# Conditioning pairs two steps earlier, VectorE's own units later, and a four-bank turn for the last heads, in a fused transformer block

## The chip, the core and the metric

The kernel runs on one core of a Trainium2 chip. The metric is device time in microseconds for one execution. Before the change the median of three runs is 1242.2 us (1241.29 to 1243.9).

## What is computed

One layer (D = 2048, 256 tokens, float32): a conditioning vector `c` gives six shift, scale and gate vectors through `w_ada`; the normalised and modulated input goes through one wide projection `w_in` into retention and attention heads; their mix goes through `w_out`; then a gated MLP with a short convolution, and a final norm with its own modulation.

```python
c_act = silu(c)
sh1, sc1, gt1, sh2, sc2, gt2 = split(c_act @ w_ada + b_ada, 6)
h = rms_norm(x, g_mix) * (1 + sc1) + sh1
rq, rk, rv, rg, aq, ak, av = split(h @ w_in + b_in)
mix = concat([retention(rq, rk, rv, rg), attention(aq, ak, av, sinks)]) @ w_out
x = x + gt1 * mix
h = rms_norm(x, g_ffn) * (1 + sc2) + sh2
a, b = split(h @ w_up)
x = x + gt2 * ((silu(conv3(a) + b_conv) * b) @ w_down)
fsh, fsc = split(c_act @ w_final_ada + b_final_ada)
y = rms_norm(x, g_final) * (1 + fsc) + fsh
```

## The kernel before

Every weight tile is split in two parts, `whi` (ScalarE, function `hi`, L661) and `wlo` (VectorE, function `lo`, L1017), and TensorE forms each product in three passes (L1546 to L1548). A piece of 128 x 1024 weights is a *step*; steps are numbered from 0 and go through TensorE in that order. Eight slots hold raw steps of the front (`front_in`), four hold the split ones. Each step of the front is one transfer of 512 KB, issued by SyncE (`load_step`, L368), and waits until the step eight before it is split (`lo_ready`).

The front, steps 0 to 51, needs the modulated input `h`, and each part of `h` needs a part of the conditioning. So the front is cut into *stages* of input tiles (`STAGE_K`: 2, 2, 4, 4, 4 tiles), and the conditioning into *jobs*. Job 0 has two parts of eight loads each (`first_units`, `first_pair`), job 1 gives the tiles of stage 2, job 2 those of stage 3, job 3 those of stage 4, job 4 a shift of the second half. A job has 16 *units* of 512 KB, loaded by GpSimd (`load_unit`, L535). TensorE takes them two at a time (`ada_pair`, L1677, eight small matmuls into bank 7 or 3); each pair counts up `ada_pe`, and GpSimd loads further units into the slots that this frees: unit 8 of job 1 waits for pair 0, and pair n of jobs 2 and 3 is asked for when the pair three before it is done (six slots). After pair 7 VectorE adds the bias (`pe_rows`, L1049), TensorE sums (`sum_columns`, L1619), VectorE forms scale and shift (`mod_cols`), and ScalarE and VectorE write the tiles of `h` of the next stage.

From job 5 on the conditioning is VectorE's own: one instruction of 1.28 us for each unit (`ada`, L1027), at the places that the table `UNIT_STEPS` gives: a number in it means that VectorE takes one unit right after `lo` of that step. Everything on one engine runs in the written order, so a unit that has not landed holds up all that is queued behind it on VectorE.

A stage has four groups of two retention heads (`two_heads`). A head takes one PSUM bank, `SPILL_BANK` says which, and VectorE adds the bank to what is kept in SBUF (`add_heads`, L1127; in stage 0 half of the heads go through `first_heads` on VectorE, L1111, and half on ScalarE). TensorE may start a head only when its bank is free (`bank_free`), that is, when VectorE or ScalarE has taken the head before it. The order of the step numbers: 0 and 2 are query steps, 1, 3, 4, 5 the heads of stage 0; 6 and 8 queries, 7, 9, 10, 11 the heads of stage 1; 12 to 23 are stage 2, 24 to 35 stage 3; 36 to 51 the rest, with the attention scores of batch 0 beside steps 44 to 47 (`att_scores`, L1811, and `scores_out` on VectorE, L1213). From step 52 on values, gates, output projection and MLP follow.

SyncE also waits for units of the conditioning between its own loads (`after_unit(job, k)`: go on when unit k of the job has landed), which sets in what order the two streams reach the DMA engines.

The functions and lines at stake:

## Time and profile before

| what | us |
|---|---|
| median of three runs | 1242.2 |
| lowest, highest | 1241.29, 1243.9 |
| the profiled execution's own time | 1238.36 |
| its span | 1236.6 |
| TensorE busy | 1182.4 (96%) |
| VectorE busy | 898.6 (73%) |

Share of the span in tenths, in 40 equal slices of 30.9 us each:

```profile
PE   5879899999999999999999999999999999999995
DVE  3334458789878797778878788787565665897886
DMA  9979899989787986788787888886565547797851
```

The span is the time from the first to the last instruction of one execution; 1.8 us of the execution's time lie around it. In the first slices TensorE is not full while the DMA engines are. A row of the timeline gives start, duration, engine, line, operation, output and inputs, shapes and the number of merged instructions; in square brackets the idle time before it and what ended it.

### The profile page before, as it was taken

What the parts mean: (1) busy time and instruction counts of PE and PEld (TensorE: products, weight loads), DVE (VectorE), ACT (ScalarE), POOL (GpSimd) and SP (SyncE); (2) the same over time, 40 slices, a digit from 0 to 9 for tenths busy, and PEclk for the clock granted to TensorE, in tenths of its full rate; (3) what the DMA queues carried; (4) which work ended last, traced back from release to release, by engine and by line L of the source; (5) the groups of instructions that cost most, each with busy time, mean ns of one, the idle gap of its engine ahead of it and who ended that gap; (6) DMA issues with size and microseconds to landing.
All of it is one profiled execution on the core that took longest, in us unless ns stands there. A gap on an engine that the chain in (4) does not pass through costs nothing.

```text
span 1236.6 us, 19629 instructions
## 1 busy us (share of the span) xinstructions
PE 1182.4 (96%) x6800; PEld 992.4 (80%) x6800; DVE 898.6 (73%) x1111; ACT 656.8 (53%) x947; POOL 180.4 (15%) x307
## 2 busy tenths in 40 slices
PE   5879899999999999999999999999999999999995
PEld 3757779876788788888888888888888887888774
DVE  3334458789878797778878788787565665897886
ACT  5313324473465446756666556566665555555652
POOL 6224132122121120011101011100000001020101
PEclk9889899999999999999999999999999999999998
DMA  9979899989787986788787888886565547797851
GB/s 314 356 281 391 299 338 328 376 341 391 283 308 282 350 311 208 237 283 292 273 292 268 292 276 283 281 279 218 174 200 175 199 181 279 273 366 258 302 180 68
DMA packets 167478, 342.73 MB, mean 277 GB/s; under 512 B 10266, under 2 KB 103552, under 8 KB 166784
## 3 DMA queue, kind: packets, MB, share of 16 engines
q1 hardware_dynamic: 129072, 206.13, 48.3%
q0 software_dynamic: 37536, 134.30, 29.4%
q10 hardware_dynamic: 816, 1.58, 0.4%
q8 instruction: 34, 0.56, 0.2%
q14 instruction: 20, 0.16, 0.0%
HBM read 339.87 MB, written 2.10 MB: 277 GB/s over the span
## 4 chain that ended last, share of the span: by engine, by line
PE 86%; DMA 6%; DVE 3%; issue 2%; ACT 1%; POOL 1%; DVEq 0%; ACTq 0%; POOLq 0%
PE ps L1570 26%; PE ps L1546 14%; PE ps L1575 14%; PE ps L1547 13%; PE ps L1548 13%; DMA arena<-in_w_ada 3%; PE ps L1677 2%; DMA ada_raw<-in_w_ada 2%; DMA raw<-in_w_in 1%; DVE acc L1027 1%; DVE xb L1344 1%; ACT whi L661 0%; POOL ada_raw L545 0%; DVE arena L1342 0%; PE ps L1852 0%
## 5 line engine op out<-in xcount | busy, mean ns | idle before, releaser
L668 ACT ACTIVATE whi<-raw 128x1024 fp32r<-128x1024 f32 x256 | 271.8, 1063 | 286.0 <-PE ps L1575 180.4
L1022 DVE TENSOR_TENSOR wlo<-raw,whi 128x1024 fp32r<-128x1024 f32 x256 | 311.8, 1223 | 104.0 <-ACT whi L668 104.0
L1570 PE MATMUL ps<-hh,whi 128*128 128x512 f32 x1408 | 353.0, 392 | 0.3 <-issue 0.3
L1570 PEld LDWEIGHTS ps<-hh,whi 128*128 128x128 f32 x1408 | 253.2, 189 | 45.8 <-issue 0.5
L1027 DVE SCALAR_TENSOR_TENSOR acc<-ada_raw,c_act,acc 128x1024 f32<-128x1024 f32 (+1 forms) x176 | 225.3, 1280 | 40.4 <-DMA ada_raw<-in_w_ada 35.0
L661 ACT ACTIVATE whi<-raw 128x1024 fp32r<-128x1024 f32 x124 | 130.6, 1059 | 217.0 <-PE ps L1548 178.2
L1546 PE MATMUL ps<-whi,hh 128*128 128x512 f32 x608 | 242.5, 399 | 1.3 <-DVE arena L1127 1.1
L1548 PE MATMUL ps<-whi,hh 128*128 128x512 f32 x608 | 237.6, 391 | 0.0
L1547 PE MATMUL ps<-wlo,hh 128*128 128x512 f32 x608 | 237.4, 391 | 0.0
L1575 PEld LDWEIGHTS ps<-hh,wlo 128*128 128x128 f32 x1408 | 192.1, 190 | 13.7
L1575 PE MATMUL ps<-hh,wlo 128*128 128x256 f32 x1408 | 196.3, 282 | 0.0
L1017 DVE TENSOR_TENSOR wlo<-raw,whi 128x1024 fp32r<-128x1024 f32 x124 | 150.8, 1220 | 60.2 <-ACT whi L661 60.2
L1546 PE MATMUL ps<-hh,whi 128*128 128x256 f32 x416 | 126.1, 303 | 22.2 <-DVE xb L1127 17.3
L1546 PEld LDWEIGHTS ps<-whi,hh 128*128 128x128 f32 x608 | 114.6, 188 | 32.4 <-issue 5.3
L535 POOL DMA_DIRECT2D ada_raw<-in_w_ada x132 | 74.0, 561 | 413.6 <-DVE acc L1027 357.1
L1548 PEld LDWEIGHTS ps<-whi,hh 128*128 128x128 f32 x608 | 114.5, 188 | 24.6
L1547 PEld LDWEIGHTS ps<-wlo,hh 128*128 128x128 f32 x608 | 114.5, 188 | 23.6 <-issue 0.7
L1547 PE MATMUL ps<-hh,whi 128*128 128x256 f32 x416 | 122.0, 293 | 0.0
L1548 PE MATMUL ps<-hh,wlo 128*128 128x256 f32 x416 | 121.9, 293 | 0.0
L1546 PEld LDWEIGHTS ps<-hh,whi 128*128 128x128 f32 x416 | 85.1, 205 | 43.7 <-issue 40.8
L1547 PEld LDWEIGHTS ps<-hh,whi 128*128 128x128 f32 x416 | 85.3, 205 | 0.0
L1548 PEld LDWEIGHTS ps<-hh,wlo 128*128 128x128 f32 x416 | 85.2, 205 | 0.0
(161 smaller groups left out, 820.4 us busy)
## 6 DMA issues: line engine op xcount, KB each, us to landing
raw<-in_w_up SPq DMA_DIRECT2D x176, 512.0 KB, 4.4
ada_raw<-in_w_ada POOLq DMA_DIRECT2D x140, 512.0 KB, 6.8
raw<-in_w_down SPq DMA_DIRECT2D x44, 1024.0 KB, 6.7
ada_raw<-in_w_final_ada POOLq DMA_DIRECT2D x64, 512.0 KB, 5.3
arena<-in_w_ada POOLq DMA_DIRECT2D x52, 512.0 KB, 8.7
raw<-in_w_in SPq DMA_DIRECT2D x52, 512.0 KB, 8.0
raw<-in_w_in SPq DMA_DIRECT2D x16, 1024.0 KB, 9.4
raw<-in_w_out SPq DMA_DIRECT2D x16, 1024.0 KB, 7.1
```

The source lines that it names most:

```text
L535: pool.dma_start(dst, src).then_inc(ada_in[slot], 16)
L661: nc.scalar.activation(whi[:, step % RING, :], raw_of(step), ACT.Copy).then_inc(hi_ready, 1)
L668: nc.scalar.activation(whi[:, i % RING, :], raw_of(step0 + i), ACT.Copy).then_inc(hi_ready, 1)
L1017: nc.vector.tensor_tensor(wlo[:, step % RING, :], raw_of(step), whi[:, step % RING, :], ALU.subtract).then_inc(lo_ready, 1)
L1022: nc.vector.tensor_tensor(wlo[:, i % RING, :], raw_of(step0 + i), whi[:, i % RING, :], ALU.subtract).then_inc(lo_ready, 1)
L1027: nc.vector.scalar_tensor_tensor(a, w, c_col, a, ALU.mult, ALU.add).then_inc(ada_acc, 1)
L1546: nc.tensor.matmul(out_ap, lhs[0], rhs[0], start=start, stop=False, skip_group_check=skip)
L1547: nc.tensor.matmul(out_ap, lhs[0], rhs[1], start=False, stop=False, skip_group_check=skip)
L1548: return nc.tensor.matmul(out_ap, lhs[1], rhs[0], start=False, stop=True, skip_group_check=skip)
L1570: nc.tensor.matmul(bank_of(m), whi[:, slot, tile(m, j)], hh[:, k0 + j, :, :].rearrange("p i s -> p (i s)"), start=start and j == 0, stop=F ...
L1575: last = nc.tensor.matmul(bank_of(m)[:, 0:S], wlo[:, slot, tile(m, j)], hhi[:, k0 + j, :], start=False, stop=True, skip_group_check=True)
L1677: last = nc.tensor.matmul(ps[row:row + 32, bank, :], c_pad[:, k, :], ada_of_slot(slot)[:, b * 512:(b + 1) * 512], start=n == 0, stop=True, ...
```

## The change

Seven edits, all in the front:

- `ada_pair(1, 0)` stands after `two_heads(0, 2, 0)` and the sums of job 0, between steps 4 and 5; it stood after step 6. Each later pair of job 1 moves with it. Its wait for `spill_dve` goes, since the heads of stage 0 no longer use bank 7.
- The heads of stage 0 take banks 5 and 6 in turn. VectorE's `first_heads(0)` stands before `lo(5)` and `lo(6)`, and `first_heads(1)` between `lo(8)` and `lo(9)`.
- SyncE issues step 5 with no wait, steps 6 and 7 after the unit 11 of job 0, step 9 with step 8, step 11 with step 10, and step 12 after unit 7 of job 1 in place of unit 12.
- VectorE's units in stage 2 move from steps 16, 18, 19, 21 to 19, 20, 23, 24, and in stage 3 from 28, 30, 31, 33, 35 to 31, 32, 34, 35, 37.
- The heads of stage 4 turn in banks 5, 6, 3, 4 instead of 5, 6, 4; the values' banks are (5, 6, 3, 4), the gates' (7, 3, 5, 6), retention's bank is 4, and the values' banks are read in the order 2, 0, 1, 3.
- `add_heads(4, ...)` of the first three groups stands after the scores of p = 7, after those of p = 9 and after the rotation of p = 11, where it stood before the scores of p = 6, of p = 8 and before the rotation of p = 10 (VectorE's p is step 42 + p).
- Nothing is computed in another way, and no instruction is added.

```diff
-SPILL_BANK = ((5, 6, 5, 6, 7, 5, 6, 7), (5, 6) * 4, (5, 6) * 4, (5, 6) * 4, (5, 6, 4, 5, 6, 4, 5, 6))
+SPILL_BANK = ((5, 6) * 4, (5, 6) * 4, (5, 6) * 4, (5, 6) * 4, (5, 6, 3, 4) * 2)
...
-AQ_BANK, AK_BANK, RV_BANKS, RG_BANKS, RET_BANK = (0, 1, 2, 4), 3, (3, 4, 5, 6), (7, 3, 4, 5), 6
+AQ_BANK, AK_BANK, RV_BANKS, RG_BANKS, RET_BANK = (0, 1, 2, 4), 3, (5, 6, 3, 4), (7, 3, 5, 6), 4
...
-UNIT_STEPS = ((16, 18, 19, 21), (28, 30, 31, 33, 35), range(38, 48), (49, 51, 53, 54), range(55, 66), (66, 66, 67, 67, 68, 69),
+UNIT_STEPS = ((19, 20, 23, 24), (31, 32, 34, 35, 37), range(38, 48), (49, 51, 53, 54), range(55, 66), (66, 66, 67, 67, 68, 69),
...
             load_heads(0, 2)
-            after_unit(0, 10)
             load_heads(0, 3)
-            after_unit(0, 13)
+            after_unit(0, 11)
             load_queries(2)
+            load_heads(1, 0)
             after_unit(0, 15)
-            load_heads(1, 0)
             load_queries(3)
-            after_unit(1, 2)
             load_heads(1, 1)
-            after_unit(1, 5)
+            after_unit(1, 3)
             load_heads(1, 2)
-            after_unit(1, 8)
             load_heads(1, 3)
-            after_unit(1, 12)
+            after_unit(1, 7)
...
-            for step in range(1, 7):
+            for step in range(1, 5):
                 lo(step)
             first_heads(0)
+            lo(5)
+            lo(6)
             first_rows(1)
             mod_cols(0, FIRST_BANKS[1], 0, 1)
             for k in STAGE_K[1]:
                 h_lo(k, 0)
+            lo(7)
+            lo(8)
             first_heads(1)
-            for step in range(7, 11):
-                lo(step)
+            lo(9)
+            lo(10)
             add_heads(1, 0)
...
-                if p in (6, 8, 10, 12):
-                    add_heads(4, p // 2 - 3)
                 if p == 12:
+                    add_heads(4, 3)
                     values_out()
...
+                    if p % 2:
+                        add_heads(4, p // 2 - 3)
...
             two_heads(0, 2, 0)
             first_sums(1)
+            ada_pair(1, 0)
             two_heads(0, 3, 0)
+            ada_pair(1, 1)

             att_queries(2)
-            ada_pair(1, 0)
+            ada_pair(1, 2)
             two_heads(1, 0, 0)
-            ada_pair(1, 1)
+            ada_pair(1, 3)
             att_queries(3)
-            ada_pair(1, 2)
+            ada_pair(1, 4)
             two_heads(1, 1, 0)
-            ada_pair(1, 3)
+            ada_pair(1, 5)
             two_heads(1, 2, 0)
-            for n in range(4, PAIRS):
-                ada_pair(1, n)
+            ada_pair(1, 6)
+            ada_pair(1, 7)
             sum_columns(1, ADA_BANK[1], 0)
             two_heads(1, 3, 0)
```

On TensorE, behind the heads of step 4, the sums of job 0 (the rows of `ones,acc`) and then step 5 stood before:

```order
L1646 MATMUL ps<-ones,acc 128x1 [waits ada_rows]
L1646 MATMUL ps<-ones,acc 128x1 x3
L1546 MATMUL ps<-hh,whi 128x256 [waits spill_dve,lo_ready,hlo_ready]
L1547 MATMUL ps<-hh,whi 128x256
L1548 MATMUL ps<-hh,wlo 128x256
```

and now, in the same place (the rows of `ada_raw,c_pad` are the first pair of job 1):

```order
L1650 MATMUL ps<-ones,acc 128x1 [waits ada_rows]
L1650 MATMUL ps<-ones,acc 128x1 x3
L1679 MATMUL ps<-ada_raw,c_pad 32x512 [waits ada_in0,mod_ready]
L1679 MATMUL ps<-ada_raw,c_pad 32x512
L1679 MATMUL ps<-ada_raw,c_pad 32x512 [waits ada_in1]
L1679 MATMUL ps<-ada_raw,c_pad 32x512
L1550 MATMUL ps<-hh,whi 128x256 [waits spill_act,lo_ready,hlo_ready]
L1551 MATMUL ps<-hh,whi 128x256
L1552 MATMUL ps<-hh,wlo 128x256
```

The pair stands before step 5, and the wait for ScalarE's head reads has taken the place of that for VectorE's.

On VectorE, in stage 2, from `lo(14)` on (`wlo` rows are `lo` of a step, `acc<-ada_raw` rows are its own units, `xb<-ps` and `gate<-ps` rows are `add_heads`), before:

```order
L1017 TENSOR_TENSOR wlo<-raw,whi 128x1024 x3
L1027 SCALAR_TENSOR_TENSOR acc<-ada_raw,c_act,acc 128x1024
L1017 TENSOR_TENSOR wlo<-raw,whi 128x1024
L1127 TENSOR_TENSOR xb<-ps,xb 128x512 x2
L1017 TENSOR_TENSOR wlo<-raw,whi 128x1024
L1027 SCALAR_TENSOR_TENSOR acc<-ada_raw,c_act,acc 128x1024
L1017 TENSOR_TENSOR wlo<-raw,whi 128x1024
L1027 SCALAR_TENSOR_TENSOR acc<-ada_raw,c_act,acc 128x1024
L1017 TENSOR_TENSOR wlo<-raw,whi 128x1024
L1127 TENSOR_TENSOR xb<-ps,xb 128x512 x2
```

and now:

```order
L1014 TENSOR_TENSOR wlo<-raw,whi 128x1024 x4
L1124 TENSOR_TENSOR xb<-ps,xb 128x512 x2
L1014 TENSOR_TENSOR wlo<-raw,whi 128x1024 x2
L1024 SCALAR_TENSOR_TENSOR acc<-ada_raw,c_act,acc 128x1024
L1014 TENSOR_TENSOR wlo<-raw,whi 128x1024
L1024 SCALAR_TENSOR_TENSOR acc<-ada_raw,c_act,acc 128x1024
L1124 TENSOR_TENSOR xb<-ps,xb 128x512 x2
L1014 TENSOR_TENSOR wlo<-raw,whi 128x1024 x3
L1024 SCALAR_TENSOR_TENSOR acc<-ada_raw,c_act,acc 128x1024
L1124 TENSOR_TENSOR gate<-ps,gate 128x512 x2
```

Ahead of the second `add_heads` of the stage (the second row of `xb<-ps`) stood three units; now two stand there, and the third follows `lo(23)`.

On VectorE, at p = 6, before (the rows of L1213 are the scores):

```order
L1017 TENSOR_TENSOR wlo<-raw,whi 128x1024
L1127 TENSOR_TENSOR arena<-ps,xb 128x512 x2
L1213 ISA arena,smx<-ps,arena 128x128
L1213 ISA smx 128x1
```

and now, at the end of p = 7 and the start of p = 8:

```order
L1214 ISA arena,smx<-ps,arena 128x128
L1214 ISA smx 128x1
L1124 TENSOR_TENSOR arena<-ps,xb 128x512 x2
L1014 TENSOR_TENSOR wlo<-raw,whi 128x1024
L1214 ISA arena,smx<-ps,arena 128x128
```

The two additions of a group of heads stand behind the scores and no longer ahead of them.

## Rows read from the trace of the kernel before

**Rows 1.** The page: busy time of TensorE; the chain that ended last, by engine.

```profile
PE 1182.4 (96%) x6800; PEld 992.4 (80%) x6800; DVE 898.6 (73%) x1111; ACT 656.8 (53%) x947; POOL 180.4 (15%) x307
PE 86%; DMA 6%; DVE 3%; issue 2%; ACT 1%; POOL 1%; DVEq 0%; ACTq 0%; POOLq 0%
```

**Rows 2.** Stretches: length, busy PE, PEld, DVE, ACT, POOL, granted clock, DMA share, GB/s.

```profile
22.90:45.70 22.80, 18.95 (x168) 15.52 (x160) 8.32 (x15) 8.71 (x14) 12.30 (x17) 0.93 1.00 350
45.70:63.20 17.50, 14.79 (x97) 13.21 (x98) 9.72 (x18) 8.39 (x13) 3.41 (x5) 0.80 0.88 323
63.20:82.60 19.40, 12.10 (x96) 9.12 (x96) 4.95 (x6) 3.18 (x3) 7.70 (x11) 0.91 0.77 271
99.40:128.60 29.20, 29.20 (x226) 21.93 (x225) 12.29 (x13) 9.54 (x10) 9.63 (x14) 0.99 1.03 391
134.80:140.80 6.00, 6.00 (x28) 5.31 (x32) 3.85 (x4) 0.50 (x1) 0.00 (x0) 0.51 0.93 315
140.80:160.00 19.20, 19.20 (x161) 17.63 (x154) 12.19 (x17) 9.52 (x14) 4.62 (x7) 1.00 0.57 187
```

**Rows 3.** Timeline of TensorE, steps 4, 10, 11 and the first pair of stage 2.

```profile
50.69 0.39 PE L1546 MATMUL ps<-hh,whi 128*128 128x256 f32 x1 [2.71 <-DVE xb L1111]
84.47 0.55 PE L1546 MATMUL ps<-hh,whi 128*128 128x256 f32 x1 [9.17 <-DVE xb L1127]
95.18 0.37 PE L1546 MATMUL ps<-hh,whi 128*128 128x256 f32 x1
102.60 1.06 PE L1677 MATMUL ps<-ada_raw,c_pad 128*32 128x512 f32 x8
```

**Rows 4.** Timelines of SyncE, ScalarE and VectorE: step 12 loaded, split in two.

```profile
76.45 0.34 SPq L368 DMA_DIRECT2D raw<-in_w_in  x1
81.41 1.06 ACT L661 ACTIVATE whi<-raw 128x1024 fp32r<-128x1024 f32 x1 [6.50 <-DMA raw<-in_w_in]
82.50 1.23 DVE L1017 TENSOR_TENSOR wlo<-raw,whi 128x1024 fp32r<-128x1024 f32 x1 [6.33 <-ACT whi L661]
```

**Rows 5.** Timelines of SyncE, ScalarE and VectorE: step 13, and job 1's bias.

```profile
82.57 0.88 SPq L368 DMA_DIRECT2D raw<-in_w_in  x2
86.51 1.06 ACT L661 ACTIVATE whi<-raw 128x1024 fp32r<-128x1024 f32 x1 [4.04 <-DMA raw<-in_w_in]
93.52 0.69 DVE L1049 TENSOR_TENSOR acc<-ps,acc 128x512 f32<-128x512 f32 x1 [2.38 <-PE ps L1677]
```

**Rows 6.** Timelines of VectorE and TensorE: units awaited, and heads that wait.

```profile
131.57 1.28 DVE L1027 SCALAR_TENSOR_TENSOR acc<-ada_raw,c_act,acc 128x1024 f32<-128x1024 f32 x1 [14.29 <-DMA ada_raw<-in_w_ada]
133.91 1.28 DVE L1127 TENSOR_TENSOR xb<-ps,xb 128x512 f32<-128x512 f32 x2
134.74 0.55 PE L1546 MATMUL ps<-hh,whi 128*128 128x256 f32 x1 [6.09 <-DVE xb L1127]
171.53 0.37 PE L1546 MATMUL ps<-hh,whi 128*128 128x256 f32 x1 [1.37 <-DVE xb L1127]
184.41 0.36 PE L1546 MATMUL ps<-hh,whi 128*128 128x256 f32 x1 [0.65 <-DVE xb L1127]
```

**Rows 7.** Timeline of TensorE: scores of batch 0 that wait for VectorE.

```profile
234.27 0.67 PE L1811 MATMUL ps<-arena 64*64 64x128 f32 x16 [0.90 <-DVE smx L1213]
243.49 0.67 PE L1811 MATMUL ps<-arena 64*64 64x128 f32 x16 [1.80 <-DVE smx L1213]
```

**Rows 8.** Timeline of TensorE: two neighbouring pairs of job 2.

```profile
118.88 1.06 PE L1677 MATMUL ps<-arena,c_pad 128*32 128x512 f32 x8
122.95 1.07 PE L1677 MATMUL ps<-arena,c_pad 128*32 128x512 f32 x8
```

**Rows 9.** DMA view of 82.6 to 201.5; GpSimd's unit loads of 30 to 140.

```profile
DMA packets 15159, 39.61 MB, mean 333 GB/s; under 512 B 1455, under 2 KB 3759, under 8 KB 15149
L535 POOL DMA_DIRECT2D ada_raw<-in_w_ada x20: 549/711/749, 33.7 to 129.7; - x20
DMA to landing us min/median/max: 3.9/8.9/15.1
```

More of the change, by code:

```diff
@@ L1247, in token_values @@
                 dve.wait_ge(step_done, STEP_RG)
-                for n in range(4):
+                for n in (2, 0, 1, 3):
                     t, b = n // 2, n % 2
@@ L1295, in _ @@
                     rotate(qT, 8 * 3 + 4, 0, p - 10)
+                if p == 11:
+                    add_heads(4, 2)
                 if p in (30, 34, 38):
@@ L1666, in ada_pair @@
                 if n == 0:
-                    if job == 1:
-                        pe.wait_ge(spill_dve, 8)
                     pe.wait_ge(mod_ready, 5 if job == JOB_SH2 else job)
@@ L1726, in bank_free @@
                 if stage == 0:
-                    return (None, None, (spill_act, 2), (spill_act, 4), (mod_ready, 1), (spill_dve, 2), (spill_dve, 4),
-                            (spill_act, 6))[n]
+                    return (None, None, (spill_act, 2), (spill_act, 4), (spill_dve, 2), (spill_dve, 4),
+                            (spill_act, 6), (spill_act, 8))[n]
                 if stage == 1 and n < 2:
-                    return ((spill_act, 8), (spill_dve, 6))[n]
+                    return spill_dve, 6 + 2 * n
                 if stage < 4 or n < 2:
                     return spill, 8 * (stage - 1) + n - 1
-                return (aq_ready, 8) if n == 2 else (spill, 8 * 3 + n - 2)
+                return ((aq_ready, 8) if n == 3 else (k2_ready, 5)) if n < 4 else (spill, 8 * 3 + n - 3)
             def two_heads(stage, group, i):
@@ L1864, in ret_values @@
                     .then_inc(o_ps, 1)
-            rv_free = [(k2_ready, 5), (spill, 30), (spill, 31), (spill, 32)]
+            rv_free = [(spill, 29), (spill, 30), (spill, 31), (spill, 32)]
             rg_free = [(mod_ready, 7), (v_ready, 1), (v_ready, 2), (v_ready, 3)]
```

## The prediction

> **What bounds the kernel now.** The page comes first. TensorE is busy for 1182.4 of 1236.6 us, and it makes 86% of the chain that ended last [rows 1]. So time can be had only where TensorE waits or runs at its lower clock, and the slices put most of that into the first 200 us. The stretches come next [rows 2]: up to 63 us and from 99 to 129 us the DMA engines move 323 to 391 GB/s and are full, but from 63.2 to 82.6 they move 271 and from 140.8 to 160.0 only 187. The front is bound by the DMA engines in turn with something that starves them. The timeline of TensorE names it. It idles 2.71 us in step 4, 9.17 us before step 10, 6.09 us before step 19, 1.37 and 0.65 us in stage 3, each time until VectorE has emptied a PSUM bank [rows 3, 6], and 0.90 and 1.80 us beside the scores [rows 7]. Behind each stands something else that VectorE waits for first: before step 10 it stands in `lo(12)`, whose data SyncE asked for only at 76.45 and which reached ScalarE at 81.41 [rows 4]; before step 19 it waits 14.29 us for a unit of its own job [rows 6]. The same waits cost clock: in the 6 us after the 6.09 us idle the granted clock is 0.51, which is the 1.2 GHz level, so some 2.9 us of those 6 are lost [rows 2, 6].
>
> **Part 1: the gate of stage 2 (pairs of job 1, SyncE's order, banks of stage 0).** Stage 2 can't start before all 16 units of job 1 have landed, been multiplied and summed. Before, SyncE issued steps 13 and on at 82.57, right behind the last unit [rows 5]. From 22.9 us on, what must land up to then is 8 loads of job 0's second part, 16 units and steps 1 to 12: 36 loads of 0.524 MB, 18.9 MB. The engines moved 350 x 22.8 = 7.98 MB and 323 x 17.5 = 5.65 MB by 63.2 [rows 2]; 5.24 MB are left. In the new order unit 8 is asked for once pair 0 is done, two steps earlier than now (6.1 us at full clock), so GpSimd's queue shouldn't run dry; at the 391 GB/s of the full stretch the rest takes 13.4 us, and the last unit lands at 76.6. If the dip at the end of the second stretch is filled as well it is 10.9 MB in 27.9 us, 73.6. If GpSimd's requests come late again it is 82.6, no gain. I take 76.6: TensorE needs until about 78 for steps 5 to 10 and eight pairs at 4.07 us for a step and a pair [rows 8], so asking and moving are nearly even.
>
> Then a new wait shows. TensorE has done pair 7 at about 78, but VectorE's `pe_rows(1)` stands behind `lo(13)`, and step 13 is still issued only when the last unit has landed. From the issue to ScalarE's start it took 3.9 us for step 13 and 5.0 for step 12, the one with units under way [rows 5, 4]; units of job 2 are under way now, so 5.0: 81.6. `hi` and `lo` end 2.3 us later (from 81.41 to 82.50 + 1.23) [rows 4], two additions take 1.2 (1.28 with their tails) [rows 6], and from `pe_rows` to step 11 it is 95.18 - 93.52 = 1.7 [rows 5, 3]. Step 11 starts at 76.6 + 5.0 + 2.3 + 1.2 + 1.7 = 86.8 instead of 95.18: 8.4 us earlier. TensorE has idled some 6 us by then. Steps 11 and 12 took 102.60 - 95.18 = 7.4 us now [rows 3], against 2 x (4.07 - 1.0) = 6.1 at full clock; after 6.09 us of idle the low clock lasted about 6 us more [rows 2], which makes up to 9.1. I take 8.5, 1.1 us worse. Part 1 gives 7.3 us, between 0 and 12.7 (73.6 and full clock). The 2.71 us wait of step 4 goes, since `first_heads(0)` no longer stands behind `lo(5)` and `lo(6)`; I count it at nothing of its own, because the DMA engines are the limit of this part. For the same reason steps 5 to 7, which SyncE asks for earlier, may make the last loads of job 0 up to 3 us late without moving the gate. The new wait of step 5 for ScalarE's head reads costs nothing: a pair of 1.06 us and the sums stand before it.
>
> **Part 2: VectorE's units in stages 2 and 3.** The third unit stood behind `lo(19)`, landed at 131.57 and held up the heads that free the bank for step 19. It now stands behind `lo(23)`, which can't run before TensorE has done step 19, 4 to 7 us behind the place where the wait hurt. Its load is still asked for after pair 4 of job 2, so in the same relation to TensorE, and lands in time by 1 to 3 us. The 6.09 us go, and with them the low clock: 2.9 us. In stage 3 the units go from steps 28, 30, 31 to 31, 32, 34, and 1.37 + 0.65 = 2.0 us go [rows 6]. No instruction is added; a unit of 1.28 us stands ahead of `mod_cols(2)` now and may make `h` 0.6 us later, hidden by two head steps of TensorE. Part 2 gives 11.0 us, between 2 and 11.
>
> **Part 3: last heads and banks.** The scores of p = 6 and p = 8 no longer stand behind two additions (1.2 us) and, at p = 8, behind a step of TensorE that isn't done. Both waits are covered by that: 0.90 + 1.80 = 2.7 us [rows 7], between 0 and 2.7. What is late next is the bank of step 50, which needs the additions of p = 9, now behind scores and maxima; they end about half a microsecond ahead of it. The values' first bank needs the additions of p = 11, done a step before it is used, and its third waits for p = 12 as now.
>
> **Part 4: what continuous running costs.** From 82.6 to 201.5 the engines moved 39.61 MB [rows 9]. At 391 GB/s that is 101.3 us, so from 76.6 it can't be done before 177.9, and TensorE would be at that point at 201.5 - 7.3 - 9.0 - 2.0 = 183.2. The margin is 5.3 us in 107. A pair of jobs 2 and 3 is asked for when the pair three before it is done, so three cycles take at least a pair, two issues of 0.71 us and the time to landing: with the median of 8.9 it is (1.07 + 1.42 + 8.9) / 3 = 3.8 us a cycle, under the 4.07 of TensorE, and from 9.7 us on the loads set the pace [rows 8, 9]. Unbroken running makes queues longer than the median. About ten pairs are paced so (five in each stage, the first three are asked for ahead). I take 10.6 us to landing, 0.3 us a pair, 3 us in all; nothing at the median, 18 us at the maximum of 15.1.
>
> **Sum.** 7.3 + 11.0 + 2.7 - 3.0 = 18.0. The profiled execution took 1238.4 (1236.6 of span and 1.8 around it), so the same execution would take 1220.4. It lies 3.8 below the median of 1242.2, and from the median I get 1224.2, about 1224.
>
> **A rule against it.** The full stretch of rows 2 shows 391 GB/s for 29 us. The Trainium skill (DMA: Bandwidth & Descriptors, Where 436 GB/s comes from) puts the limit for loads from HBM at about 358 GB/s for a core. By that page's figure, as an estimate, the 39.61 MB would need 110.6 us and end at 187.2, 4.0 us behind TensorE, which is close to the 3.0 of part 4. The trace doesn't agree with the page on the rate; it would have to fall with a longer full stretch.
>
> The trace shows step 12 landing 5 us after its issue with units under way and step 13 after 3.9 [rows 4, 5]. The Trainium skill (the same page, Queues, rings and completion order) says that each DMA engine takes turns between the queues that have work, so an earlier step of SyncE takes its share from the units whoever asked first. By that rule the early steps 5 to 7 delay job 0's last loads, which the sum takes at nothing because the total of bytes up to the gate is the same.
>
> **Rivals.** *The loads set the pace.* Landing takes about 12.5 us when nothing pauses: 5.0 us a pair, 0.93 x 10 = 9 us lost instead of 3. For it: the full stretch had 391 GB/s with no reserve. Against it: TensorE was busy for all 29.2 us of it. Time 1242.2 - 21.0 + 9.3 = 1230.5.
>
> *All gaps close.* The gate lands at 73.6, the clock stays up, no pair waits: 12.7 + 11.0 + 2.7 = 26.4, 1215.8. Against it: the wait behind step 13 is long enough for the clock to fall.
>
> *The gate doesn't move.* The early steps push back the loads that pair 0 needs and the last unit still lands near 82; then only parts 2 and 3 less part 4 are left, 10.7: 1231.5. For it: unit 8 can't be asked for before pair 0, and pair 0 stands behind all of job 0's loads. Against it: at 271 GB/s the engines had room from 63.2 to 82.6 [rows 2].
>
> *Slower.* The ring of six slots, with landing beyond what was seen. The gains make 21.0 at most by the sum, so ten pairs have to lose 2.1 us each, which starts at 3 x 6.17 - 2.5 = 16.0 us to landing. At 17 us it is 6.5 us a pair, 24 lost, 1245.5. The longest landing now is 15.1 [rows 9], of a unit queued behind others, so only if every load became like the worst.
>
> **Chances.** Forecast 0.58, the loads set the pace 0.18, all gaps close 0.11, the gate doesn't move 0.07, slower 0.06. The predicted time is 1224, its own range 1219 to 1229. The range for 8 in 10 takes in most of both neighbours: 1214 to 1233. About 0.2% (2.5 us) is what a measurement can tell from no change. Faster 0.91, same 0.03 (small parts of two rivals), slower 0.06.
>
> **What would show it.** No idle before step 10 ended by VectorE; one wait of 4 to 7 us instead, before the sums of job 1, behind `lo(13)`, with the low clock after it; step 11 near 87 and the first pair of stage 2 near 95. No 6 us wait in stage 2, and none on VectorE above a few us for its third unit; 375 to 390 GB/s where 187 was. Pairs of jobs 2 and 3 ended by a DMA, some tenths each. The scores' waits gone. I am wrong if step 11 starts after 92, if pairs in stage 2 follow each other at 4.6 us or more, or if a new wait on VectorE stands before steps 48 to 52.

## The result

The changed kernel takes 1221.19 us (median of four runs, 1220.77 to 1223.63) against 1241.74 (1237.94 to 1243.9, four runs): ratio 0.9842, 95% interval 0.9814 to 0.9869. The prediction was 1224, 1214 to 1233. In the profiled executions the span went from 1236.6 to 1219.6, 17.0 us; the prediction's sum was 18.0. The four runs of one kernel lie 3 to 6 us apart, so below the sizes of single parts are read from the profiles, at the same instruction in both.

The page of the changed kernel: the span, the busy time, and TensorE and the DMA engines in 40 slices.

```profile
span 1219.6 us, 19628 instructions
PE 1177.9 (97%) x6800; PEld 986.6 (81%) x6800; DVE 899.0 (74%) x1111; ACT 656.4 (54%) x947; POOL 180.6 (15%) x307
PE   5979999999999999999999999999999999999995
DMA  9999999999688894888878788886555457897841
```

TensorE's busy time fell by 4.5 us with the same 6800 matmuls: that is clock. The other 12.5 us are idle time that went. The DMA engines are now busy for 90% or more in each of the first ten slices.

Four stretches of the changed kernel (length, busy PE, PEld, DVE, ACT, POOL, granted clock, DMA share, GB/s), beside those of [rows 2]:

```profile
45.70:63.20 17.50, 15.96 (x134) 12.62 (x131) 10.16 (x17) 7.40 (x12) 7.70 (x11) 1.00 1.03 388
63.20:76.30 13.10, 12.26 (x99) 9.31 (x98) 6.08 (x7) 3.17 (x3) 4.88 (x7) 1.00 0.95 354
76.30:143.00 66.70, 59.94 (x456) 49.57 (x455) 35.99 (x46) 24.23 (x32) 19.95 (x29) 0.92 0.99 369
85.80:96.00 10.20, 10.20 (x56) 10.09 (x56) 5.00 (x10) 5.76 (x10) 1.46 (x2) 0.63 1.03 393
```

Where 323 GB/s were moved from 45.7 to 63.2 us at a clock of 0.80, there are 388 at full clock now (a second profile of the changed kernel, e10 below, has 388 at a clock of 0.90). After the gate of stage 2 the clock is low again, 0.63 for 10 us.

TensorE's timeline of the changed kernel, in the place of [rows 3]: step 10, pairs 6 and 7 of job 1, its sums, the first pair of stage 2.

```profile
74.06 0.36 PE L1550 MATMUL ps<-hh,whi 128*128 128x256 f32 x1 [0.84 <-DVE xb L1124]
77.11 1.92 PE L1679 MATMUL ps<-arena,c_pad 128*32 128x512 f32 x16
85.80 1.87 PE L1623 MATMUL ps<-pick,acc 128*128 128x2 f32 x8 [6.76 <-DVE acc L1046]
96.02 1.07 PE L1679 MATMUL ps<-ada_raw,c_pad 128*32 128x512 f32 x8
```

The 9.17 us before step 10 are 0.84. In their place stand 6.76 us before the sums. What VectorE did in that time is the chain forecast, in the places of [rows 4, 5] (SyncE, ScalarE, VectorE):

```profile
76.33 1.98 SPq L368 DMA_DIRECT2D raw<-in_w_in  x3
...
81.63 1.06 ACT L658 ACTIVATE whi<-raw 128x1024 fp32r<-128x1024 f32 x1 [9.58 <-DMA raw<-in_w_in]
...
82.72 1.23 DVE L1014 TENSOR_TENSOR wlo<-raw,whi 128x1024 fp32r<-128x1024 f32 x1 [8.21 <-ACT whi L658]
83.86 0.68 DVE L1124 TENSOR_TENSOR gate<-ps,gate 128x512 f32<-128x512 f32 x1
85.06 0.68 DVE L1046 TENSOR_TENSOR acc<-ps,acc 128x512 f32<-128x512 f32 x1
```

The last unit landed at 76.3, SyncE issued step 13 behind it, `lo(13)` could start at 82.72, and the bias of job 1 stood behind that, at 85.06.

VectorE's third unit, in the place of [rows 6], has no wait at all (no brackets):

```profile
126.90 1.28 DVE L1024 SCALAR_TENSOR_TENSOR acc<-ada_raw,c_act,acc 128x1024 f32<-128x1024 f32 x1
```

New are waits of TensorE for the DMA engines in stages 3 and 4: before the second half of pairs 6 and 7 of job 3, and of the pair beside step 45.

```profile
167.45 1.05 PE L1679 MATMUL ps<-arena,c_pad 128*32 128x512 f32 x4 [1.02 <-DMA arena<-in_w_ada]
...
173.32 1.05 PE L1679 MATMUL ps<-ada_raw,c_pad 128*32 128x512 f32 x4 [0.76 <-DMA ada_raw<-in_w_ada]
...
219.70 1.05 PE L1679 MATMUL ps<-arena,c_pad 128*32 128x512 f32 x4 [0.96 <-DMA arena<-in_w_ada]
...
228.04 0.67 PE L1815 MATMUL ps<-arena 64*64 64x128 f32 x16
```

The last row is the place of the second wait of [rows 7]; it and the first are gone.

Starts in the two profiles, and what each stretch gave:

| place | before | after | gained up to here | in the stretch |
|---|---|---|---|---|
| first pair of stage 2 | 102.60 | 96.02 | 6.6 | 6.6 |
| first pair of stage 3 | 156.89 | 140.98 | 15.9 | 9.3 |
| sums of job 3 | 194.43 | 180.17 | 14.3 | -1.7 |
| first step of the values | 261.05 | 245.67 | 15.4 | 1.1 |
| end of the span | 1236.6 | 1219.6 | 17.0 | 1.6 |

In the second profile of the changed kernel the same places lie at 97.6, 143.0, 182.3, 248.05 and 1224.3. There the last stretch is 0.7 us longer than in the kernel before, so the 1.6 us of the last line are no gain of the change.

### The profile page after: what moved, and what is told of

It reads as the page before. It is cut to its first block, busy times and chain, and to the rows that moved or that the text cites. A ratio compares the mean times of both kernels' runs of the same rounds, so it can differ in the third digit from the quotient of the medians.

```text
span 1219.6 us, 19628 instructions
## 1 busy us (share of the span) xinstructions
PE 1177.9 (97%) x6800; PEld 986.6 (81%) x6800; DVE 899.0 (74%) x1111; ACT 656.4 (54%) x947; POOL 180.6 (15%) x307
## 4 chain that ended last, share of the span: by engine, by line
PE 87%; DMA 7%; DVE 2%; issue 1%; POOL 1%; ACT 1%; DVEq 0%; ACTq 0%; POOLq 0%
PE ps L1574 27%; PE ps L1550 14%; PE ps L1579 14%; PE ps L1552 14%; PE ps L1551 14%; DMA arena<-in_w_ada 4%; PE ps L1679 2%; DMA ada_raw<-in_w_ada 2%; DMA raw<-in_w_in 1%; DVE xb L1348 1%; POOL ada_raw L542 1%; DVE arena L1346 0%; PE ps L1856 0%; PE ps L1955 0%; PE ps L1641 0%
## 5 line engine op out<-in xcount | busy, mean ns | idle before, releaser
L1574 PEld LDWEIGHTS ps<-hh,whi 128*128 128x128 f32 x1408 | 253.2, 189 | 45.7 <-issue 0.4
L1579 PEld LDWEIGHTS ps<-hh,wlo 128*128 128x128 f32 x1408 | 192.1, 190 | 13.7
L1550 PE MATMUL ps<-hh,whi 128*128 128x256 f32 x416 | 123.4, 297 | 3.1 <-DVE hh L1075 2.3
L1551 PE MATMUL ps<-hh,whi 128*128 128x256 f32 x416 | 119.5, 287 | 0.0
L1550 PEld LDWEIGHTS ps<-hh,whi 128*128 128x128 f32 x416 | 82.5, 198 | 25.7 <-issue 25.7
L1552 PEld LDWEIGHTS ps<-hh,wlo 128*128 128x128 f32 x416 | 82.6, 199 | 0.0
L1551 PEld LDWEIGHTS ps<-hh,whi 128*128 128x128 f32 x416 | 82.6, 198 | 0.0
```

The costliest lines, as they stand in the source:

```text
L1550: nc.tensor.matmul(out_ap, lhs[0], rhs[0], start=start, stop=False, skip_group_check=skip)
L1551: nc.tensor.matmul(out_ap, lhs[0], rhs[1], start=False, stop=False, skip_group_check=skip)
L1552: return nc.tensor.matmul(out_ap, lhs[1], rhs[0], start=False, stop=True, skip_group_check=skip)
L1574: nc.tensor.matmul(bank_of(m), whi[:, slot, tile(m, j)], hh[:, k0 + j, :, :].rearrange("p i s -> p (i s)"), start=start and j == 0, stop=F ...
L1579: last = nc.tensor.matmul(bank_of(m)[:, 0:S], wlo[:, slot, tile(m, j)], hhi[:, k0 + j, :], start=False, stop=True, skip_group_check=True)
```

## The experiments

Each of them is told by its ratio to the kernel before, since its runs went beside that kernel's, and by the start of the first pair of stage 2 and of the first pair of stage 3. For the changed kernel these are 96.0 and 141.0; a second profile of it had 97.6 and 143.0, and two of the kernels below, in which nothing ahead of the gate is altered, had 97.9 and 95.9. So profiles of the same front differ there by 2 us of themselves, and a difference of 2 us between two kernels says nothing.

**e1: VectorE's units at their old steps.**

```diff
-UNIT_STEPS = ((19, 20, 23, 24), (31, 32, 34, 35, 37),
+UNIT_STEPS = ((16, 18, 19, 21), (28, 30, 31, 33, 35),
```

> The changed kernel with VectorE's units back at steps 16, 18, 19, 21 and 28, 30, 31, 33, 35. Theory (part 2 of the prediction): the third unit, asked for at about 115 us and landed at about 125, holds up the additions before step 19 again: TensorE idles about 6 us in stage 2, its clock falls after it, and stage 3 has its two small waits on VectorE; 1221 + 9 to 11 = 1230 to 1232. Rival (the loads set the pace in stages 2 and 3, and moving the units mattered little): the idle only takes the place of the waits of the last two pairs of job 3 (3.9 us in the changed kernel); 1221 + 0 to 5.

1228.14 us, ratio 0.9914 (0.9891 to 0.9938). TensorE before step 19 and in stage 3:

```profile
130.14 0.56 PE L1550 MATMUL ps<-hh,whi 128*128 128x256 f32 x1 [6.51 <-DVE xb L1124]
...
165.94 0.36 PE L1550 MATMUL ps<-hh,whi 128*128 128x256 f32 x1 [0.86 <-DVE xb L1124]
...
181.15 0.36 PE L1550 MATMUL ps<-hh,whi 128*128 128x256 f32 x1 [2.97 <-DVE xb L1124]
```

All three waits are back, and the pairs' waits for the DMA engines are gone. From the first pair of stage 2 to the first of stage 3 it is 151.8 - 97.9 = 53.9 us against 45.0 in the changed kernel: 9 us. The whole costs 0.6 to 0.7%, or 7 to 9 us, a little under the 9 to 11 expected. In stage 3 nothing is lost: from its first pair to the sums of job 3 it is 191.06 - 151.80 = 39.3 us against 39.2 in the changed kernel. The waits for VectorE there only stand in the place of those for the DMA engines.

**e6: the units alone, in the kernel before** (the same two lines, the other way).

> The kernel before with only VectorE's units moved to steps 19, 20, 23, 24 and 31, 32, 34, 35, 37. Theory (part 2): the 6.09 us idle in stage 2, the low clock behind it and the two small idles of stage 3 go, 11 us; the loads of the last pairs of job 3 make TensorE wait for 2 to 4 us, so 7 to 9 us faster than the kernel before. From the profile: the first pair of stage 2 stays at about 102.6, the first of stage 3 is at about 147.5 instead of 156.9. Rival (moving them pays only behind an earlier gate): under 4 us.

1234.53 us, ratio 0.9951 (0.9923 to 0.9979), about 6 us where 7 to 9 were expected. The stretch between the two first pairs is 150.3 - 102.9 = 47.4, 6.9 less than before; the two pairs wait for the DMA engines as in the changed kernel:

```profile
176.41 1.05 PE L1677 MATMUL ps<-arena,c_pad 128*32 128x512 f32 x4 [0.67 <-DMA arena<-in_w_ada]
...
182.19 1.05 PE L1677 MATMUL ps<-ada_raw,c_pad 128*32 128x512 f32 x4 [0.67 <-DMA ada_raw<-in_w_ada]
```

Part 2 stands by itself. The first pair of stage 3 came 2.8 us later than expected: some pairs of stage 2 were stretched too (the one at 115.13 took 2.19 us instead of 1.07).

**e2: the pairs of job 1 at their old places.**

```diff
             first_sums(1)
-            ada_pair(1, 0)
             two_heads(0, 3, 0)
-            ada_pair(1, 1)
             att_queries(2)
-            ada_pair(1, 2)
+            ada_pair(1, 0)
...
```

> The changed kernel with the pairs of job 1 at their old places (pair 0 after step 6), the loads of SyncE in the new order. Theory (the gate is set by how early unit 8 can be asked for): the last unit of job 1 lands at 81 to 83 instead of 76.3, pe_rows of job 1 starts at about 91, the first pair of stage 2 at about 101 instead of 96.0; 1225 to 1227. Rival (SyncE's earlier loads alone fill the engines, the pair's place matters little): the last unit lands before 78, 1221 to 1223.

1223.28 us, ratio 0.9887 (0.9844 to 0.9931). The last unit landed at 77.9, the first pair of stage 2 started at 97.2. The theory expected 81 to 83 and about 101; the rival holds for the gate. The place of the pairs alone is not what moved it.

**e3: SyncE's loads in the old order.**

```diff
-            load_heads(0, 3)
-            after_unit(0, 11)
+            after_unit(0, 10)
+            load_heads(0, 3)
+            after_unit(0, 13)
             load_queries(2)
...
```

> The changed kernel with SyncE's loads of steps 5 to 12 behind the same units as in the kernel before. Theory (the engines are full up to the gate, the total of bytes is what counts): the last unit of job 1 lands within 1.5 us of 76.3, and the time is 1220 to 1224. But step 12 then waits for unit 12 of job 1, which lands at about 72.4, so it lands near 77 and the additions behind lo(12) that step 10 needs come at about 79.5: TensorE idles some 5 us before step 10. Since the gate (pe_rows near 85) is later than that, two pairs after step 10 have to follow in 2 us; the time is then 1222 to 1226. Rival (the order of the loads is what brought the gain of the gate): over 1228.

1222.72 us (1219.49 to 1228.15), ratio 0.9888 (0.984 to 0.9935). Step 13 was issued at 75.3, so the last unit had landed, 1 us earlier than in the changed kernel. TensorE waits before step 10 as expected, but hardly before the sums:

```profile
79.62 0.55 PE L1553 MATMUL ps<-hh,whi 128*128 128x256 f32 x1 [5.16 <-DVE xb L1127]
...
87.65 1.05 PE L1626 MATMUL ps<-pick,acc 128*128 128x2 f32 x8 [0.89 <-DVE acc L1049]
...
94.50 1.06 PE L1682 MATMUL ps<-ada_raw,c_pad 128*32 128x512 f32 x8
```

The sums come 1.9 us later than in the changed kernel and the first pair of stage 2 comes 1.5 us earlier: from one to the other it is 6.9 us at full clock, where the changed kernel, at 0.63, needs 10.2. So the idle of 6.76 us cost 3.3 us more in clock, half its own length. In e3 the low clock came too, but from 78 to 84.7 us, ahead of the sums.

**e7: both undone.** The edits of e2 and e3 together.

> The changed kernel with both the pairs of job 1 and SyncE's loads of steps 5 to 12 at their old places; banks, VectorE's order and units stay new. Alone, each of the two moved the start of stage 2 by about 1 us (97.2 and 94.5 against 96.0). Theory (each of the two is enough to keep the DMA engines full up to the gate): without both the last unit lands at 81 to 83, the wait of 9 us before step 10 is back, and the first pair of stage 2 starts at 100 to 103; 1226 to 1229. Rival (what moved the gate is the new place of first_heads on VectorE and the banks of stage 0, which end the idle of step 4): the first pair starts before 98, 1221 to 1224.

1226.61 us, ratio 0.9884 (0.9857 to 0.9911). The last unit landed at 78.0, where 81 to 83 was expected; the wait before step 10 is back, and the first pair of stage 2 starts at 98.1, between the two theories:

```profile
79.81 0.55 PE L1553 MATMUL ps<-hh,whi 128*128 128x256 f32 x1 [8.65 <-DVE xb L1127]
...
89.76 1.05 PE L1626 MATMUL ps<-pick,acc 128*128 128x2 f32 x8 [0.89 <-DVE acc L1049]
...
98.10 1.07 PE L1682 MATMUL ps<-ada_raw,c_pad 128*32 128x512 f32 x8
```

Against the mean of the four profiles with the changed front (96.0, 97.6, 97.9, 95.9: 96.9) pairs and loads together are worth 1.2 us here. The ratio says 0.3 to 0.4% of the whole time, 4 to 5 us, with intervals that overlap.

**e9: in the kernel before, only stage 0's banks and VectorE's order there.**

```diff
-SPILL_BANK = ((5, 6, 5, 6, 7, 5, 6, 7),
+SPILL_BANK = ((5, 6) * 4,
...
-            for step in range(1, 7):
+            for step in range(1, 5):
                 lo(step)
             first_heads(0)
+            lo(5)
+            lo(6)
...
-                    if job == 1:
-                        pe.wait_ge(spill_dve, 8)
```

> The kernel before with only stage 0's banks (5 and 6 in turn) and VectorE's first_heads in front of lo(5) and behind lo(8); pairs, loads, units and last heads stay as before. The kernel with pairs and loads both undone had its first pair of stage 2 at 98.1, where the kernel before has 102.6. Theory (most of the gate's gain came from the end of the 2.71 us idle in step 4 and of the low clock behind it, since every later request for units hangs on TensorE's progress): pair 0 of job 1 at about 58 instead of 62.0, its last unit at about 78 instead of 82.6, the first pair of stage 2 at 98 to 99; the 6 us idle of stage 2 stays; 3 to 5 us faster than before. Rival (this edit only helps beside the earlier pairs, as the prediction had it): the first pair of stage 2 within 1 us of 102.6, no gain that can be measured.

1236.32 us (12 runs), ratio 0.998 (0.996 to 1.0), some 2.5 us. Pair 0 of job 1 started at 60.6 instead of 62.0, the last unit landed at 80.0, the first pair of stage 2 started at 100.0:

```profile
52.21 1.16 PE L1650 MATMUL ps<-ones,acc 128*128 128x1 f32 x8 [2.10 <-DVE acc L1042]
...
84.33 0.55 PE L1550 MATMUL ps<-hh,whi 128*128 128x256 f32 x1 [10.51 <-DVE xb L1127]
...
99.99 1.07 PE L1679 MATMUL ps<-ada_raw,c_pad 128*32 128x512 f32 x8
```

About half of what was expected, and between theory and rival. The first row says why: the wait of 2.71 us in step 4 is gone, but one of 2.10 us stands before the sums of job 0 instead, since VectorE's bias is queued behind `lo(6)` and step 6 landed late. The clock is low behind it again (0.50 from 54 to 56 us).

e7 and e9 have the same front in every line that comes ahead of the gate. Their profiles lie 1.9 us apart there, 4.6 and 2.7 us ahead of the mean of the kernel before and e6 (102.6, 102.9). Of the 5.9 us between that mean and 96.9, banks and VectorE's order in stage 0 thus gave 2.7 to 4.6, and pairs and loads together the other 1.2 to 3.2. The times of the runs lean the other way (e9 gains 0.2%, e7 lacks 0.3 to 0.4%). So both count, and which counts for more is open. Banks and VectorE's order were not tried apart either.

**e4: the last heads as before** (banks of stage 4, values, gates and retention, and the places of `add_heads(4, ...)`).

```diff
-SPILL_BANK = ((5, 6) * 4, (5, 6) * 4, (5, 6) * 4, (5, 6) * 4, (5, 6, 3, 4) * 2)
+SPILL_BANK = ((5, 6) * 4, (5, 6) * 4, (5, 6) * 4, (5, 6) * 4, (5, 6, 4, 5, 6, 4, 5, 6))
...
+                if p in (6, 8, 10, 12):
+                    add_heads(4, p // 2 - 3)
```

> The changed kernel with the heads of stage 4, their additions and the banks of values, gates and retention as before. Theory (part 3): the waits of the scores for VectorE are back, about 0.9 and 1.8 us, but the pair of p = 3, whose unit lands late (0.96 us idle in the changed kernel), then waits less; from the scores of p = 2 to the first step of the values 1 to 2.5 us are lost, 1222 to 1224. Rival (the loads of job 4's pairs set the pace there): no loss, 1220 to 1222.

1223.01 us (1221.64 to 1225.13), ratio 0.9856 (0.9826 to 0.9885): not told apart from the changed kernel by its runs. Its profile shows one of the two waits and the late unit:

```profile
219.29 1.05 PE L1676 MATMUL ps<-arena,c_pad 128*32 128x512 f32 x4 [0.77 <-DMA arena<-in_w_ada]
229.50 0.67 PE L1812 MATMUL ps<-arena 64*64 64x128 f32 x16 [1.80 <-DVE smx L1214]
```

From the sums of job 3 to the first step of the values it needs 247.05 - 179.95 = 67.1 us against 245.67 - 180.17 = 65.5: by these two profiles part 3 is worth 1.6 us, not 2.7. The second profile of the changed kernel has 65.7 and that of e7, with the new last heads, 66.4, so it may be as little as 0.7.

**e5 and e11: steps 13 and 14 loaded ahead of SyncE's wait for the last unit** (one kernel, run twice).

```diff
                     load_queries(STAGE_K[stage][group])
+                    load_heads(stage, group)
                     if stage == 2 and group == 0:
                         after_unit(1, 15)
-                    load_heads(stage, group)
```

> The changed kernel with steps 13 and 14 loaded right behind step 12, ahead of SyncE's wait for the last unit of job 1. Theory (pe_rows of job 1 stands behind lo(13), whose load is issued only when the last unit has landed, and that is the 6.8 us idle before the sums): two more transfers of 1.35 us come before the last unit, which lands at about 79; pair 7 ends at 80, pe_rows starts at about 81 instead of 85.06, TensorE idles under 3 us, its clock stays up for steps 11 and 12 (2 to 3 us more), and the first pair of stage 2 starts at 89 to 91 instead of 96.0; the time is 1214 to 1217. Rival (what is gained at the gate is lost to the loads of stages 2 and 3, which are the bound from 76 to 165 us): the waits of the last pairs of job 3 grow by as much, 1219 to 1222.

1219.06 us (1216.4 to 1220.84), ratio 0.9836 (0.9795 to 0.9878): the time that the rival expected, while the first pair of stage 2, at 88.5, came as early as the theory had it, or earlier. **e10** is the changed kernel again and **e11** this version again, side by side:

> The changed kernel as it is, in the same call as the next one. Theory and rival: 0.984 of the kernel before, as measured; its first pair of stage 2 within 1 us of 96.0.

> The version that loads steps 13 and 14 ahead of the wait for the last unit of job 1, beside the changed kernel on the same chip. Theory (7.5 us gained at the gate, of which the full DMA engines of stages 2 and 3 and a longer stretch of low clock near 300 us take all but some): 1 to 3 us below the changed kernel. Rival (all of it is given back): within 1 us of it.

The changed kernel took 1222.63 us (1219.14 to 1225.98), ratio 0.9851 (0.9824 to 0.9878); this version 1217.2 (1215.63 to 1219.41), ratio 0.9824 (0.9799 to 0.985), five runs each. Side by side this version is 5.4 us faster than the changed kernel, more than the 1 to 3 expected. By the ratios it is 0.3% there and 0.1% for e5, with intervals that overlap, so how much it gains isn't settled. What it did at the gate is (rows of e11):

```profile
81.07 1.05 PE L1623 MATMUL ps<-pick,acc 128*128 128x2 f32 x8 [0.86 <-DVE acc L1046]
...
87.91 1.07 PE L1679 MATMUL ps<-ada_raw,c_pad 128*32 128x512 f32 x8
...
102.33 1.05 PE L1679 MATMUL ps<-ada_raw,c_pad 128*32 128x512 f32 x4 [1.16 <-DMA ada_raw<-in_w_ada]
...
162.31 1.05 PE L1679 MATMUL ps<-arena,c_pad 128*32 128x512 f32 x4 [0.52 <-DMA arena<-in_w_ada]
...
168.74 1.05 PE L1679 MATMUL ps<-ada_raw,c_pad 128*32 128x512 f32 x4 [1.24 <-DMA ada_raw<-in_w_ada]
```

The idle before the sums is 0.86, the clock stays at 1.00, and the first pair of stage 2 is 8.1 us earlier. At the first pair of stage 3 (136.34 against 140.98) 4.6 of that are left. The rest went into waits for the DMA engines, which run at 384 GB/s without a break from 78 to 143:

```profile
78.00:143.00 65.00, 62.97 (x485) 49.72 (x482) 36.41 (x46) 24.01 (x32) 22.43 (x33) 1.00 1.02 384
```

**e8: VectorE's units behind the pairs**, on top of that version: GpSimd asks for units 5, 6, 7 behind pair 7 of job 3, and VectorE takes them later.

```diff
-                if n in (3, 5, 6, 7):
-                    dve_unit({3: 4, 5: 5, 6: 6, 7: 7}[n])
+                if n == 3:
+                    dve_unit(4)
+            dve_unit(5)
+            dve_unit(6)
+            dve_unit(7)
...
-UNIT_STEPS = ((19, 20, 23, 24), (31, 32, 34, 35, 37),
+UNIT_STEPS = ((19, 20, 23, 24), (31, 35, 36, 37, 37),
```

> The version with steps 13 and 14 loaded ahead of the wait for the last unit of job 1, and GpSimd asks for VectorE's units 5, 6 and 7 only behind the last pair of job 3; VectorE takes them at steps 35, 36, 37, 37 instead of 32, 34, 35, 37. Theory (the pairs 6 and 7 of job 3 wait because two units and SyncE's steps are queued ahead of them on full DMA engines): their waits (0.7 and 0.95 us idle, 3.3 us with what each costs) shrink to under 1 us together, the sums of job 3 start at 173 to 174.5 instead of 176.1; 1216 to 1218. Rival (whatever lies ahead, the engines are short of bytes up to there, and the units come due later): the wait moves to VectorE's units before the sums of job 3 or the h of stage 4, and the time is 1218 to 1222.

1221.05 us (1219.46 to 1221.7), ratio 0.9837 (0.9809 to 0.9864), no better than e5 and e11. The pairs 6 and 7 wait no more and the sums of job 3 start at 172.5, earlier than expected; then the waits stand elsewhere:

```profile
185.73 0.36 PE L1553 MATMUL ps<-hh,whi 128*128 128x256 f32 x1 [0.69 <-DVE wlo L1017]
192.71 0.36 PE L1553 MATMUL ps<-hh,whi 128*128 128x256 f32 x1 [1.00 <-DVE wlo L1017]
214.32 1.05 PE L1682 MATMUL ps<-arena,c_pad 128*32 128x512 f32 x4 [2.12 <-DMA arena<-in_w_ada]
216.89 1.92 PE L1682 MATMUL ps<-arena,c_pad 128*32 128x512 f32 x4 [1.52 <-DMA arena<-in_w_ada]
```

The rival holds. Asking for the pairs' loads ahead of VectorE's units moved the wait, it didn't end it.

**e12: that version with the pairs at their old places.**

> The version with steps 13 and 14 loaded early, and the pairs of job 1 at their old places. Theory (the earlier pairs are worth something only when the sums don't wait for lo(13)): the last unit lands at 81 to 82 instead of 79.1 to 79.7, pairs 4 to 7 come bunched behind step 10, the sums start at 83 to 85 instead of 81.1 to 81.7, the first pair of stage 2 at 90 to 92 instead of 87.9 to 88.5; half of that is given back to the full DMA engines, 1218 to 1220 against 1217.2. Rival (the pairs' place is worth nothing there either): sums before 82.5, within 1 us of 1217.2.

1220.56 us (1218.81 to 1221.8), ratio 0.9862 (0.984 to 0.9884). The sums start at 80.45 and the first pair of stage 2 at 87.3, earlier than with the pairs early: the theory is wrong, and the rival is right about the gate. About the time it isn't: the profile's span is 3.2 us longer than e11's, with the waits of pair 7 of job 3 at 1.05 and 1.03 us in its two halves and a stretch of low clock at 299 us that e11 hasn't. But e5's profile, of the same kernel as e11, has a low clock there too (0.74 from 300 to 310) and a span of 1219.1, longer than e12's 1217.1. Whether the early pairs gave e11 its time, or single runs just fall differently, is open.

## Why the prediction was right, and where it wasn't

*The time and its sum.* 18.0 us were forecast, 17.0 came in the profile, and the medians give 20.6 here and 17.8 in e10. By the table the parts came to 6.6 at the gate (7.3 forecast), 9.3 in stage 2 (9.0), -1.7 in stage 3 (2.0 less 3.0) and 1.1 at the last heads (2.7), 15.4 together. The 1.6 us that bring it to 17.0 belong to no part of the forecast, and e10 doesn't have them: that they fill the gap is luck.

*The chain at the gate* was right link by link. The last unit at 76.6 (76.3), step 13 at ScalarE at 81.6 (81.63), the bias behind `lo(13)` at 85.1 (85.06), low clock behind it, the first pair of stage 2 at 95.3 (96.02; 97.6 in the second profile). The idle was 6.76 us where some 6 were expected. e5 shows that this wait is what its description says: with step 13 loaded earlier it is 0.86.

*The size of the earlier gate* was met partly by luck. The sum kept 323 GB/s up to 63.2 us and took 391 from there. The engines moved 388 and then 354 GB/s, and the two differences nearly cancel: the last unit landed at 76.3 (78.0 in e10) though the dip was filled, a case for which the prediction had 73.6. Loading steps 5 to 7 early also had its price: TensorE waits 1.53 us for the last pair of job 0 (0.53 before), within the 3 us that the prediction allowed.

*The cause of the earlier gate* was wrong in part. The prediction counted the 2.71 us of step 4 "at nothing of its own", "because the DMA engines are the limit of this part", and gave the whole gain to the requests. The failing step is that reason. In the kernel before, the engines were full only up to 56 us, and the share of 0.88 in [rows 2] said so already:

```profile
45.70:56.00 10.30, 7.59 (x49) 6.98 (x50) 5.30 (x10) 4.92 (x9) 3.41 (x5) 0.80 1.03 391
56.00:63.20 7.20, 7.20 (x50) 6.23 (x49) 4.42 (x9) 3.48 (x5) 0.00 (x0) 0.80 0.66 226
```

Every request for units 8 to 15 hangs on a pair of TensorE, so the idle of 2.71 us and the low clock behind it delayed requests: in e7, where both are gone, pair 0 of job 1 starts at 57.9 instead of 62.0 at its old place. e9 and e7 show that banks and VectorE's order in stage 0, with pairs and loads at their old places, bring the gate forward by 2.7 and 4.6 us. Pairs and loads at their old places move the first pair of stage 2 by 0.3 (e2), -2.4 (e3) and 1.2 us (e7, both) against the mean of 96.9, not by 7.

But the end of that idle doesn't fill the engines by itself. From 45.7 to 63.2 us (e9, then e7):

```profile
45.70:63.20 17.50, 14.87 (x113) 13.13 (x110) 10.52 (x18) 7.51 (x12) 4.66 (x7) 0.90 0.91 336
45.70:63.20 17.50, 16.94 (x144) 14.04 (x143) 10.92 (x18) 8.55 (x13) 4.88 (x7) 1.00 0.97 352
```

With the early loads alone it is 383 GB/s (e2), with the early pairs alone 388 (e3), with both 388. So either of the two is enough to fill them, and for the rate the other adds little. The rate is not all of it: the last unit landed at 77.9 in e2, as in e7 (78.0). What the early pairs then bring to the gate ends in the wait behind `lo(13)` and its low clock: e7, with its sums 4.0 us later, has its first pair only 2.1 later.

*Part 2* was forecast at 9.0 us in stage 2 and came to 9.3; e1 gives 9 back, and alone (e6) it is 6.9. In stage 3 the waits of 2.0 us went as forecast, but the waits for the DMA engines took their place: e1, which has them back, needs the same 39.3 us for that stretch.

*Part 4* was forecast at 3.0 us spread over ten pairs. The mechanism (the ring of six slots, with landing slower than 9.7 us) was right and the place was off: nearly all of it stands at pairs 6 and 7 of job 3. From the first pair of stage 3 to the sums it is 39.2 us against 37.5 before, in which 2.0 were waits for VectorE, so the new waits cost 3.7. GpSimd's loads into `ada_raw` from 150 to 160 us in the changed kernel, of which those of pair 7 are two, landed so:

```profile
L532 POOL DMA_DIRECT2D ada_raw<-in_w_ada x4: 567/638/711, 151.9 to 159.4; - x4
DMA to landing us min/median/max: 10.1/12.1/13.9
```

The prediction's rival in which the loads set the pace took 12.5 us to landing for all pairs; something near it holds for the last two of stage 3 only.

*Part 3* was forecast at 2.7 and is 0.7 to 1.6 by e4. Both waits are gone, but only the second was there to be won: e4, e6 and e9, with the old last heads, have the 1.80 us and not the 0.90. In its place the pair beside step 45 waits 0.77 us (e4) and 1.38 us (e6) for its second unit, as it does in the changed kernel (0.96); in e9 that wait is 0.20. The prediction counted both waits as covered and didn't ask what else was late there.

*The rule against it.* From 76.3 to 143 the engines moved 369 GB/s at a share of 0.99, and in e11 384 GB/s over 65 us. The figure of about 358 GB/s for loads from HBM (the Trainium skill, DMA: Bandwidth & Descriptors, Where 436 GB/s comes from) is not a limit here over 65 us either.

## What to carry to other kernels

Idle time of the engine whose progress releases the next loads can cost time even in a stretch where the DMA engines look full: it delays the requests, and here it took the clock with it. Look at such a stretch in finer slices before calling it full: 323 GB/s over 17.5 us were 391 for ten and 226 for the rest. Before crediting an earlier request with a gain, undo it alone and with its neighbours; here pairs and loads could each stand in for the other, and a reordering priced at nothing gave 3 to 5 of the 6 us by the profiles. When the waits have gone from an engine, look at the queue order in front of the next one (here a load held behind a wait for other data), and at the bytes: where the DMA engines ran without a break (e8), moving one load ahead of another only moved the wait.

## What was not expected of the hardware

The clock fell some time after an idle began and stayed down after work had resumed. In the changed kernel TensorE stopped at 79.0 us; the granted clock was 1.00 until 83, 0.50 (the 1.2 GHz level) from 84 to 93, though TensorE worked again from 85.8 on, and 1.00 from 94. The 10.2 us up to the first pair of stage 2 ran at 0.63; in e3, with 5.16 us of idle before step 10 and 0.89 before the sums, the same instructions took 6.9 us at full clock. So the place of an idle, not only its length, decides which work pays for it.

Single runs of one kernel differ by up to 7 us (1219.1 to 1226.0 for the changed kernel), and e9's twelve runs by 13.7. Part of that is which of the early instructions fall into low clock. The two profiles of the changed kernel show it: in the first, a wait of 1.53 us for the last pair of job 0 cost no clock; in the second, 1.68 us in the same place were followed by 0.50 from 50 to 53 us. Pair 0 of job 1 started at 51.8 and 54.9, and the first pair of stage 2 still lay 1.6 us apart.
